# Upper and lower token parts in one 512-column matmul, in a feed-forward's up projection

## What is computed

```python
def sq_relu_mlp(h, w_up, w_down):
    u = jnp.matmul(h, w_up)                       # (256, 1024) x (1024, 4096)
    return jnp.matmul(jnp.square(jax.nn.relu(u)), w_down)

h = rms_norm(x, mlp_pre_g[layer])
x = x + rms_norm(sq_relu_mlp(h, w_up[layer], w_down[layer]), mlp_post_g[layer])
```

## Time and profile before

| | |
|---|---|
| median of 3 runs | 1111.68 us (1111.32 to 1112.38) |
| the profiled execution | 1110.63 us, of which the span 1108.8 us |
| TensorE, matmuls busy | 951.5 us (86% of the span) |
| VectorE busy | 483.0 us (44%) |
| ScalarE busy | 386.1 us (35%) |
| chain that ended last | PE 69%, DMA 18%, DVE 7%, ACT 3% |
| mean granted TensorE clock | 0.935 |

### The profile page before, as it was taken

How to read it: one execution, slowest core, us unless ns; L and a number is a source line. 1 busy time by engine, 2 the same in 40 slices (tenths; PEclk the granted TensorE clock), 3 DMA queues, 4 the chain that set the end, 5 groups by cost and what they waited for, 6 DMA issues and landing times.

```text
span 1108.8 us, 14786 instructions
## 1 busy us (share of the span) xinstructions
PE 951.5 (86%) x5959; PEld 710.0 (64%) x5959; DVE 483.0 (44%) x806; ACT 386.1 (35%) x697; POOL 1.9 (0%) x7
## 2 busy tenths in 40 slices
PE   8999999999999999999999899859393867666657
PEld 6899899889778989998789774414151414132232
DVE  5656655765557655666757853201101010202020
ACT  4655544663766544555655531000000000000000
POOL 0000000000000000000000000000000000000000
PEclk9999999999999999999999999979796888888879
DMA  9745454644224355455340999999999999999996
GB/s 351 291 152 213 168 224 152 218 161 172 76 77 171 152 195 184 161 218 176 128 152 21 357 390 378 429 427 430 426 427 428 429 429 429 429 427 429 428 421 257
DMA packets 63425, 309.95 MB, mean 280 GB/s; under 512 B 2704, under 2 KB 3728, under 8 KB 53136
## 3 DMA queue, kind: packets, MB, share of 16 engines
q1 hardware_dynamic: 62944, 307.68, 70.1%
q0 software_dynamic: 432, 1.57, 0.4%
HBM read 308.19 MB, written 1.05 MB: 279 GB/s over the span
## 4 chain that ended last, share of the span: by engine, by line
PE 69%; DMA 18%; DVE 7%; ACT 3%; issue 1%; SPq 1%; DVEq 0%; ACTq 0%
PE ps L680 14%; DMA ring<-in_w_exp_down 14%; PE ps L681 14%; PE ps L682 14%; PE ps L1142 7%; PE ps L1189 6%; PE ps L1124 5%; DMA ring<-in_w_exp_up 3%; PE ps L1201 2%; DVE w_lo L1761 1%; PE ps L875 1%; DVE w_lo L1748 1%; DMA scale_row<-in_pool_scale 1%; DVE hT_lo L1742 1%; SPq L636 1%
## 5 line engine op out<-in xcount | busy, mean ns | idle before, releaser
L1748 DVE TENSOR_TENSOR w_lo<-ring,w_hi 128x1024 fp32r<-128x1024 f32 x158 | 190.4, 1222 | 76.1 <-ACT w_hi L1303 76.1
L1142 PE MATMUL ps<-ring,x 128*32 128x512 f32 x992 | 129.6, 680 | 72.3 <-DMA ring<-in_w_exp_up 63.1
L1303 ACT ACTIVATE w_hi<-ring 128x1024 fp32r<-128x1024 f32 x158 | 164.0, 1053 | 74.8 <-PE ps L682 74.6
L680 PE MATMUL ps<-hT_hi,w_hi 128*128 128x256 f32 x656 | 186.9, 285 | 2.9 <-DVE hT_lo L1742 2.1
L682 PE MATMUL ps<-hT_hi,w_lo 128*128 128x256 f32 x656 | 185.6, 283 | 0.0
L681 PE MATMUL ps<-hT_lo,w_hi 128*128 128x256 f32 x656 | 185.6, 283 | 0.0
L1142 PEld LDWEIGHTS ps<-ring,x 128*32 128x32 f32 x992 | 37.5, 123 | 157.2 <-issue 155.7
L680 PEld LDWEIGHTS ps<-hT_hi,w_hi 128*128 128x128 f32 x656 | 125.8, 192 | 4.8 <-DVE w_lo L1748 2.9
L681 PEld LDWEIGHTS ps<-hT_lo,w_hi 128*128 128x128 f32 x656 | 125.8, 192 | 0.6
L682 PEld LDWEIGHTS ps<-hT_hi,w_lo 128*128 128x128 f32 x656 | 125.8, 192 | 0.0
L1189 PE MATMUL ps<-ring,moe 128*32 128x512 f32 x512 | 70.3, 708 | 56.2 <-DMA ring<-in_w_exp_down 54.8
(11 more groups left out here) (286 smaller groups left out, 1180.6 us busy)
## 6 DMA issues: line engine op xcount, KB each, us to landing
ring<-in_w_exp_gate SPq DMA_DIRECT2D x31, 2048.0 KB, 20.0
ring<-in_w_exp_up SPq DMA_DIRECT2D x31, 2048.0 KB, 20.6
ring<-in_w_exp_down SPq DMA_DIRECT2D x31, 2048.0 KB, 18.2
ring<-in_w_up SPq DMA_DIRECT2D x16, 2048.0 KB, 8.0
ring<-in_w_down SPq DMA_DIRECT2D x16, 2048.0 KB, 7.6
ring<-in_w_in SPq DMA_DIRECT2D x6, 2048.0 KB, 8.3
ring<-in_w_kv SPq DMA_DIRECT2D x4, 2048.0 KB, 10.3
ring<-in_w_q SPq DMA_DIRECT2D x2, 2048.0 KB, 9.9
```

Of the source, the lines that this page charges most:

```text
L680: mm(out, a_hi, b_hi, start=start, stop=False, skip_group_check=True)
L1142: last = mm(wk(side)[q, :], xgT[:, k, q], w4[:, j, k % 2, :] if opening else w[j][:, k, :], start=(k == 0), stop=(k == KD - 1))
L1303: fn(parts(n if edge else None, f)[0].rearrange("p (k w) -> p k w", k=KD), src, ACT.Copy).then_inc(hi_ready, 1)
L1748: ve.tensor_tensor(lo, src, hi.bitcast(F32), ALU.subtract).then_inc(lo_ready, 1)
```

## The change

The lower token part is laid directly behind the upper one in a common tile `hT`, so that one matmul can take both as 512 moving columns: for each k a new helper `both_columns` multiplies `w_hi` by upper and lower token parts (512 columns, one half of the bank for each), and `w_lo` by the upper part (256 columns, added to the first half). A quarter has 16 matmuls in place of 24. The sum over both halves is made behind it: ScalarE copies the second half from PSUM to `rT` (`second_part`), VectorE adds the first half out of PSUM to it, and the ReLU, which read PSUM, now works within `rT`. In `step` both engines do `second_part` ahead of the split of the quarter two further on. Two semaphores are new.

```diff
--- before.py
+++ after.py
@@ -221,8 +221,8 @@
         w_lo = at("w_lo", [P, 4, 1024], w_base + 16 * K, F32R)
         mixT_hi = at("mixT_hi", [P, KD, T], w_base + 32 * K, F32R)
         mixT_lo = at("mixT_lo", [P, KD, T], w_base + 40 * K, F32R)
-        hT_hi = at("hT_hi", [P, KD, T], w_base + 48 * K, F32R)
-        hT_lo = at("hT_lo", [P, KD, T], w_base + 56 * K, F32R)
+        hT = at("hT", [P, 2, KD, T], w_base + 48 * K, F32R)
+        hT_hi, hT_lo = (hT[:, i, :, :] for i in range(2))
         ring2 = at("ring2", [P, RING, CHUNK], w_base)
         yT = at("yT", [P, KD, T], w_base + 32 * K)
 
@@ -380,6 +380,8 @@
         mix_r0 = sem("mix_r0")
         mg_ready = sem("mg_ready")
         r2_ready = sem("r2_ready")
+        up_copied = sem("up_copied")
+        up_summed = sem("up_summed")
         relu_ready = sem("relu_ready")
         sq_hi = sem("sq_hi")
         sq_full = sem("sq_full")
@@ -727,6 +729,17 @@
                     last = mm3(out, [q[:, k, :] for q in w], [q[:, k, :] for q in ops], k == 0, k == KD - 1)
                 last.then_inc(quarters_used, 1)
 
+            def both_columns(out, b, turn=None, n=None):
+
+                w = [q.rearrange("p (k w) -> p k w", k=KD) for q in parts(n, b)]
+                for k in range(KD):
+                    if turn is not None and k % 2 == 0:
+                        pe.wait_ge(hT_lo_ready, 8 * turn + 4 + k // 2 + 1)
+                    mm(out.rearrange("p (b t) -> p b t", b=2), w[0][:, k, :], hT[:, :, k, :], start=k == 0, stop=k == KD - 1,
+                       skip_group_check=True)
+                    last = mm(out[:, 0:T], w[1][:, k, :], hT_hi[:, k, :], start=False, stop=k == KD - 1, skip_group_check=True)
+                last.then_inc(quarters_used, 1)
+
             def token_major(outs, n, f):
 
                 for kk in range(2):
@@ -769,7 +782,7 @@
                 def up(j, i):
                     for f in range(4):
                         split(n0 + 2 * j, f, i)
-                        channel_major(wk(f)[:, 0:T], f, (hT_hi, hT_lo))
+                        both_columns(wk(f), f)
 
                 def down(j, i, closing=False):
 
@@ -795,7 +808,7 @@
                 keep_busy(7, (6, 3)[layer])
                 for f in range(4):
                     split(n0, f)
-                    channel_major(wk(f)[:, 0:T], f, (hT_hi, hT_lo), turn if f == 0 else None, n0)
+                    both_columns(wk(f), f, turn if f == 0 else None, n0)
                 for s in range(TT):
                     for half in range(2):
                         mm(acc[:, s, half * COLS:(half + 1) * COLS], zero_t[:, 0:P], zero_t[:, 0:COLS],
@@ -1380,22 +1393,28 @@
             def mlp(layer):
                 n0 = N_MLP[layer]
 
+                def second_part(j, f, i):
+
+                    act.wait_ge(quarters_used, i * QI + (4 * (n0 + j) + f + 1))
+                    fn(rT[:, f, :], wk(f)[:, T:2 * T], ACT.Copy).then_inc(up_copied, 1)
+
                 def square(j, f, i):
-                    n = n0 + j
-
-                    act.wait_ge(quarters_used, i * QI + (4 * n + f + 1))
-                    fn(rT[:, f, :], wk(f)[:, 0:T], ACT.Relu).then_inc(relu_ready, 1)
+                    act.wait_ge(up_summed, i * (4 * PAIRS) + (32 * layer + 4 * (j // 2) + f + 1))
+                    fn(rT[:, f, :], rT[:, f, :], ACT.Relu).then_inc(relu_ready, 1)
                     act.wait_ge(relu_ready, i * (4 * PAIRS) + (32 * layer + 4 * (j // 2) + f + 1))
                     fn(aT_hi[:, f, :], rT[:, f, :], ACT.Square).then_inc(sq_hi, 1)
 
                 def step(j, f, i):
+                    if j % 2 == 0:
+                        second_part(j, f, i)
                     n2, f2 = ahead_of(n0 + j, f)
                     split(n2, f2, mlp_quarter(n2, n2 - n0, f2), i)
                     if j % 2 == 0:
                         square(j, f, i)
 
-                square(0, 0, 0)
-                square(0, 1, 0)
+                for f in range(2):
+                    second_part(0, f, 0)
+                    square(0, f, 0)
                 step(0, 2, 0)
                 step(0, 3, 0)
                 with act.Fori(0, PAIR_ITERS - 1) as i:
@@ -1405,6 +1424,7 @@
                     for f in range(4):
                         if f < 2:
 
+                            second_part(0, f, i + 1)
                             n2, f2 = ahead_of(n0, f)
                             split(n2, f2, mlp_quarter(n2, 0, f2), i + 1, False)
                             square(0, f, i + 1)
@@ -1857,6 +1877,11 @@
             def mlp(layer):
                 n0 = N_MLP[layer]
 
+                def second_part(j, f, i):
+                    done = 32 * layer + 4 * (j // 2) + f
+                    dve.wait_ge(up_copied, i * (4 * PAIRS) + (done + 1))
+                    ve.tensor_tensor(rT[:, f, :], wk(f)[:, 0:T], rT[:, f, :], ALU.add).then_inc(up_summed, 1)
+
                 def square(j, f, i):
                     done = 32 * layer + 4 * (j // 2) + f
                     dve.wait_ge(relu_ready, i * (4 * PAIRS) + (done + 1))
```

## The result

| | before | with the change |
|---|---|---|
| median | 1112.29 us (1111.32 to 1114.16, 7 runs) | 1116.63 us (1116.03 to 1117.78, 7 runs) |
| profiled execution, span | 1110.63 us, 1108.8 us | 1116.85 us, 1114.9 us |

A forecast was written before the change was run, and what follows sets the result against it. TensorE was taken to bound both feed-forwards. Loop pairs -0.8, last pairs -0.1, layer ends +2.8, layer 1's start -0.4 and layer 0's +0.7 sum to +2.2 us: 1113.9 us on the median, range 1109.0 to 1119.0.

The forecast's parts named there:

- the 22.3 to 22.5 named as a sign: Feed-forward loop: if the forecast is right, one pair of up and down projections repeats every 22.3 to 22.5 us.
- TensorE is the bound and work on the other engines fits beside it: Feed-forwards: TensorE always busy; per 2.78 us up quarter VectorE has 2.5 us of work, ScalarE 2.3, at no cost.
- The chain from E to the streaming of the quarter two further on, w = 2.93 us: From an up quarter's end (E), through copy, both split parts and weight load, to matmuls two quarters on: 2.93 us.
- It is the order that costs: Feed-forward loop: the copy ahead of the split waits for the up quarter's end, so TensorE waits some 0.15 us.
- A new wait of 1.42 us at each layer's end: Before the second down quarter of each layer's last down projection: TensorE newly waits 1.42 us, 2.8 in all.
- Starts: Each layer's first four up quarters: layer 1 gains 0.4 us, layer 0 loses 0.7 because ScalarE is late.
- The up quarter, u = 2.777 us: Up projection: with matmuls of 0.227 and 0.120 us per k, a quarter takes 2.777 us, 0.103 less than before.
- the forecast of -0.054 per pair: Loop, one up and down projection: 4 x -0.103 + 2 x 0.153 + 0.052 = -0.054 us; -0.8 for 14 pairs.
- The bounds of 0.213 and 0.240 us for the merged matmul: Up projection's 512-column matmul: 0.213 us for columns alone at 2.4 GHz, 0.240 if nothing is saved; priced at 0.227.
- rival C: Up projection: merging saves nothing, the matmul over two pieces takes 0.240 us; +7.0 us, 1118.7 us; chance 0.14.
- Rival D: Chain from quarter's end 0.2 us longer, by register instructions or two engines reading PSUM: 5.6 us more, 1119.5 us; chance 0.14.
- Rival B: Loop: the split is in time and TensorE's waits vanish; -2.8 us, 1108.9 us; chance 0.14.

The follow-up runs named there:

- the mixed order: The changed kernel with ScalarE's split put back ahead of its copy, VectorE's addition still ahead of the lower part's split: 1112.19 us, ratio 0.9999 to the kernel before.
- both splits first: The changed kernel with the split put back ahead of the copy on ScalarE and of the addition on VectorE: 1127.60 us, ratio 1.0124 to the kernel before.

## Why the prediction was right, and where it was short

The time, 1116.63 us, lies in the range (1109.0 to 1119.0), and the sign was right, slower; the forecast of +2.2 us is half of the +4.3 measured. It lies above 1112.5 to 1115.5, the narrower range given for the mechanism that came true, and the pair's period of 22.56 us lies just outside the 22.3 to 22.5 named as a sign. By its own steps:

- *TensorE is the bound and work on the other engines fits beside it*: right. Three matmuls with all the added work in the mixed order have the old period of 22.42 us. The engines' busy time grew by 18 and 17 us, not the 27 forecast, as the forecast added up durations that overlap.
- *The chain from E to the streaming of the quarter two further on, w = 2.93 us*: measured 2.95. (The forecast has the lower part begin 1.57 us after E in one place, where its own links add up to 1.55; nothing hangs on it.) *It is the order that costs*: shown by the ReLU put ahead of the split, with 6.7 us for no work at all, about 6 expected.
- *A new wait of 1.42 us at each layer's end*: measured 1.43 and 1.42 us.
- *Starts*: -0.4 in layer 1, measured -0.40; in layer 0 +0.7, measured +0.46, since the two chains did take the 4.0 us of the text, but started 0.25 us earlier: ScalarE's first three copies start at 36.30, 38.58 and 40.34 us, the first of them not at the 36.55 of the earlier trace rows.
- *The up quarter, u = 2.777 us*: this is **the term that was mis-sized**. In the first chunks it holds exactly (0.3467 us per k). In the loops, 14 of 16 pairs, a k took 0.3533 us in quarters 0 to 2 and 0.347 to 0.351 in quarter 3: a 512-column matmul beside 256-column ones took 233 to 241 ns, not the 227 of the down projection. The forecast's sum per pair counts u three times, for quarters 0, 2 and 3, since quarter 1 ends inside the wait before quarter 2. Quarters 0 and 2 took 0.05 us more each and quarter 3 about 0.01, 0.11 us per pair or 1.5 us in all; w, 0.02 longer twice, adds 0.6. With both, the forecast of -0.054 per pair becomes +0.10; measured were +0.14 in layer 0 and +0.12 in layer 1. That closes 2.1 of the 2.5 us between the forecast and the table's 4.7. The Trainium skill, "TensorE: Matmul & The Clock Gate", section "Back-to-back issue gap", gives N/2.4 ns plus 2.5 ns as the gap of a single matmul, and by that a merger would save 2.5 ns per k. These rows disagree: against the 0.360 us of before, it saved 13.3 ns per k in the first chunks and 6.7 in the loops.
- *The bounds of 0.213 and 0.240 us for the merged matmul* held on the average (0.237; single starts reach 0.241), and rival C named the right direction with a wrong cause: the two pieces are innocent. Rival D (a chain 0.2 us longer) came in a small part only: the 0.08 us more before down 0 in 10 of 14 pairs, most of which takes the place of the wait before down 1. Why it stands only in TensorE's loop no run tests; register instructions are D's own guess. Rival B (no wait in the loop) is what the mixed order brings.

The text did not look at what the added addition does to the dependences *between* the two engines. In the order of the change it does no harm, but the obvious repair, both splits first, closes a ring of 3.45 us, and only a run showed it.

## What to carry to other kernels

On engines that work in order, ask of each added instruction what it waits for and what stands behind it, before you ask how long it takes: here the same 0.8 us of added work per quarter was free in the loop and cost 2 to 3 us at the starts and ends of the layers, or cost 15 us per execution, by its place alone. Follow the chain through both engines for one full turn, since the split ahead on ScalarE with the sum ahead on VectorE leaves it open, where the split ahead on both closes a ring. And try the order of matmuls of two lengths: with the waits gone, the merged matmul strictly alternating with the short one gave the time of before (0.9999), and only with the order turned for odd k or with the eight long ones in one run did it pay, by 0.2 to 0.4%.

## What the runs showed that was not expected

The time between matmul starts depends on the neighbours' lengths. In a uniform stream it was 227 ns (512 columns) and 120 ns (256), all at a granted clock of 1.00 (2.4 GHz). Strictly alternating, the same program ran in one of two rhythms, 346.7 ns per k (the change's first chunks) or 353.3 ns (quarters 0 to 2 of its loops; with both splits first and in the mixed order the first chunks too). Turned for odd k it took 348.5 ns; grouped 346 in quarter 0 and 349 in the others, no less on the whole. After a change from 256 to 512 columns about five starts were 228 to 236 ns before 227 came back; the kernel before shows that too, at the start of each down projection. Which of the two rhythms a stream falls into, and why, was not settled: moving columns in one piece do not matter, and neither does the work of ScalarE and VectorE, as the slow rhythm stood in quarter 0, where both sat idle.
